# Weight slots of a split-precision transformer kernel: raw 6 to 4, high and low parts 3 to 4

## The reference

```python
for l in range(DEPTH):                      # DEPTH = 2, first block
    h = rmsnorm(x, norm_mix[l])
    proj = h @ w_in[l]                      # 1024 x 5956
    ...                                     # rope, top-k attention, recurrence
    merged = sigmoid(ga) * (y_attn @ w_proj_attn[l]) + sigmoid(gb) * (y_hgrn @ w_proj_hgrn[l])
    x = x + merged @ w_out[l]
    g, u = split(rmsnorm(x, norm_ffn[l]) @ w_ffn_in[l])     # 1024 x 5632
    x = x + (silu(g) * u) @ w_ffn_out[l]                    # 2816 x 1024
mod = silu(c) @ ada_w + ada_b               # second block: 1024 x 6144
...
x = x + g1 * rms_norm(hybrid_mixer(...))
x = x + g2 * rms_norm(swiglu_ffn(...))
```

## Time and profile before

| what | us |
|---|---|
| median of 3 runs | 1318.49 |
| the runs | 1316.56 to 1318.83 |
| the profiled execution, its own time | 1319.73 |
| span of that execution | 1317.9 |
| PE busy | 1213.8 |
| DVE busy | 849.3 |
| ACT busy | 616.0 |

### The profile page before, as it was taken

How to read it: one execution, slowest core, us unless ns; L and a number is a source line. 1 busy time by engine, 2 the same in 40 slices (tenths; PEclk the granted TensorE clock), 3 DMA queues, 4 the chain that set the end, 5 groups by cost and what they waited for, 6 DMA issues and landing times.

```text
span 1317.9 us, 21169 instructions
## 1 busy us (share of the span) xinstructions
PE 1213.8 (92%) x9046; PEld 1164.0 (88%) x9046; DVE 849.3 (64%) x1272; ACT 616.0 (47%) x738; POOL 0.2 (0%) x4
## 2 busy tenths in 40 slices
PE   5888978899999999789789999999899998999996
PEld 5678978899999987789789999999797887899996
DVE  6984463777676788844637776767775647644443
ACT  7565315464334355653154643343564347443343
POOL 0000000000000000000000000000000000000000
PEclk9999989999999999999899999999898798999998
DMA  9454322565868663544325658786443203455510
GB/s 346 124 174 128 128 96 65 170 214 173 273 228 278 212 207 91 179 128 128 96 65 179 205 178 270 240 273 214 154 146 110 96 1 128 160 189 171 184 65 33
DMA packets 177614, 214.15 MB, mean 162 GB/s; under 512 B 3696, under 2 KB 160752, under 8 KB 177520
## 3 DMA queue, kind: packets, MB, share of 16 engines
q1 hardware_dynamic: 176800, 211.86, 48.7%
q10 hardware_dynamic: 720, 0.94, 0.2%
HBM read 211.74 MB, written 1.05 MB: 161 GB/s over the span
## 4 chain that ended last, share of the span: by engine, by line
PE 72%; DVE 16%; ACT 8%; issue 3%; DMA 1%; SPq 0%; DVEq 0%; ACTq 0%
PE stream L492 16%; PE stream L493 15%; PE stream L494 15%; DVE w_lo L1304 6%; PE steps L494 4%; PE steps L493 4%; PE steps L492 4%; ACT w_hi L881 4%; PE steps L799 2%; PE steps L657 1%; PE stream L676 1%; ACT probs L881 1%; PE stream L580 1%; DMA raw<-in_w_in 1%; PE steps L647 1%
## 5 line engine op out<-in xcount | busy, mean ns | idle before, releaser
L1304 DVE TENSOR_TENSOR w_lo<-raw,w_hi 128x2048 fp32r<-128x2048 f32 (+2 forms) x178 | 402.4, 2266 | 328.2 <-ACT w_hi L881 326.5
L881 ACT ACTIVATE w_hi<-raw 128x2048 fp32r<-128x2048 f32 (+2 forms) x178 | 336.6, 1894 | 415.1 <-PE stream L494 372.0
L492 PE MATMUL stream<-h_hi,w_hi 128*128 128x256 f32 x1576 | 454.4, 288 | 11.7 <-DVE w_lo L1304 6.0
L493 PE MATMUL stream<-h_lo,w_hi 128*128 128x256 f32 x1576 | 449.9, 285 | 0.0
L494 PE MATMUL stream<-h_hi,w_lo 128*128 128x256 f32 x1576 | 449.6, 285 | 0.0
L492 PEld LDWEIGHTS stream<-h_hi,w_hi 128*128 128x128 f32 x1576 | 307.0, 195 | 15.5 <-DVE w_lo L1304 7.8
L493 PEld LDWEIGHTS stream<-h_lo,w_hi 128*128 128x128 f32 x1576 | 306.9, 195 | 0.5 <-issue 0.5
L494 PEld LDWEIGHTS stream<-h_hi,w_lo 128*128 128x128 f32 x1576 | 306.5, 195 | 0.0
L492 PE MATMUL steps<-gu_hi,w_hi 128*128 128x256 f32 x528 | 149.5, 283 | 0.7 <-DVE gu_lo L1561 0.7
L493 PE MATMUL steps<-gu_lo,w_hi 128*128 128x256 f32 x528 | 149.4, 283 | 0.0
L494 PE MATMUL steps<-gu_hi,w_lo 128*128 128x256 f32 x528 | 149.4, 283 | 0.0
(11 more groups left out here) (286 smaller groups left out, 1706.7 us busy)
## 6 DMA issues: line engine op xcount, KB each, us to landing
raw<-in_w_ffn_in SPq DMA_DIRECT2D x66, 1024.0 KB, 5.2
raw<-in_w_in SPq DMA_DIRECT2D x54, 1024.0 KB, 6.0
raw<-in_w_ffn_out SPq DMA_DIRECT2D x33, 1024.0 KB, 6.7
ada_raw<-in_ada_w SPq DMA_DIRECT2D x24, 1024.0 KB, 5.3
raw<-in_w_out SPq DMA_DIRECT2D x8, 1024.0 KB, 5.0
raw<-in_w_proj_attn SPq DMA_DIRECT2D x8, 512.0 KB, 3.5
raw<-in_w_proj_hgrn SPq DMA_DIRECT2D x8, 512.0 KB, 4.6
raw<-in_w_o SPq DMA_DIRECT2D x4, 1024.0 KB, 4.9
```

Source lines behind the costliest of these rows:

```text
L492: pe.matmul(dst, w_h, x_h, start=start, stop=False, skip_group_check=True)
L493: pe.matmul(dst, w_h, x_l, start=False, stop=False, skip_group_check=True)
L881: return act.activation(out_, in_, func, **kw)
L1304: tt(wl[m % SPL][:, 0:n], raw[m % RAW][:, 0:n], wh[m % SPL][:, 0:n].bitcast(F32), ALU.subtract)\
```

## The change

The raw slots go from six to four, the high and low parts from three to four each. The memory is the same 96 KB of each partition, cut otherwise. `split_ahead()` now splits the unit four places ahead. Since one more unit has to be ready at the start, `mixer(0)` gets one more split on each engine: on ACT behind a wait for parameters, on DVE behind `setup_tables()`. `first_outs` keeps working on three units. SP's loads wait for the split of the unit four before rather than six before.

```diff
-RAW = 6
-SPL = 3
+RAW = 4
+SPL = 4
...
-    wh = [at(f"w_hi{i}", [P, 2048], F32R, 48 + 8 * i) for i in range(SPL)]
-    wl = [at(f"w_lo{i}", [P, 2048], F32R, 72 + 8 * i) for i in range(SPL)]
+    wh = [at(f"w_hi{i}", [P, 2048], F32R, 32 + 8 * i) for i in range(SPL)]
+    wl = [at(f"w_lo{i}", [P, 2048], F32R, 64 + 8 * i) for i in range(SPL)]
...
             m = cur[0]
-            cur[0] += SPL
+            cur[0] += 3
...
-            for i in range(SPL):
+            for i in range(3):
...
                 split(2)
                 act.wait_ge(par_in, 64)
+                split(3)
             step()
             split_ahead()
...
                 setup_rope()
                 split(2)
                 setup_tables()
+                split(3)
```

## The result

| | before | changed |
|---|---|---|
| median of the runs, us | 1318.47 (1316.56 to 1318.83, 4 runs) | 1327.2 (1327.11 to 1328.34, 4 runs) |
| ratio | | 1.0071, 95% interval 1.0054 to 1.0089 |
| profiled execution, us (its span) | 1319.73 (1317.9) | 1327.29 (1325.5) |
| mean granted clock of TensorE | 0.953 | 0.946 |

The changed kernel is 8.7 us (0.7%) slower. I had forecast +4.7 us, with 1326.5 us as the upper end of the range. The sign was right. The time lies 0.7 us outside the range.

What follows compares the result with a forecast made beforehand. The prediction took PE to set the time over most of the kernel and DVE in two stretches. Its terms, 2.7 + 2.3 + 0.8 - 1.1 = +4.7 us, gave 1323.2 us on the median, range 1320.0 to 1326.5 us.

Steps and rivals of the forecast that it cites:

- What bounds the kernel: PE over most of the kernel, DVE in two stretches; PE's 10.6 us of `w_lo` waits there taken as worth 0 us.
- Rival (a): In DVE's two stretches, the extra ready unit pays: PE regains 10.6 us, net -5.9, 1312.6 us; chance 7%.
- what stays: PE's stops for something behind a split on DVE, for example in the recurrence, stay as they are; no change in time.
- First and second term: At the start, ACT's added split delays the cosine by 2.7 us; DVE's added split delays the rotation by 2.3 us more.
- rival (c): At the start, unit 4 lands late, its packets mixed with unit 5's: +7.4 us, 1325.9 us; chance 12%.
- Both terms go to the end: The start's 2.7 and 2.3 us pass through DVE to PE's softmax stop and the kernel's end: +5.0 us.
- rival (b): DVE's extra split at the start, 2.3 us, is hidden before the first softmax: +2.4 us, 1320.9 us; chance 15%.
- Third term: At block 0's end, the split ahead of the additions to `xT` grows from 1.50 to 2.29 us: +0.8 us.
- Fourth term: At block 1's end, the split ahead of the additions to `xT` shrinks from 2.28 to 1.22 us: -1.1 us.
- The loads: Loads issued two units later still land in time in the feed-forward parts: 0 us.
- Rival (d): Loads come too late in the feed-forward parts: +10 us and more, 1333 us; chance 3%.

Runs made afterwards that it cites:

- the pair with the decays first: DVE's two decays of each recurrence level moved ahead of that level's split, nothing else: 1290.7 us on the kernel before (three slots), 1302.4 us on the changed kernel (four).
- The pure delay on the kernel before: The kernel before with DVE's six writes of the rope tables made six times over instead of once, slots and splits untouched: 1326.0 us, ratio 1.0053.

## Why the prediction was right or wrong

- **What bounds the kernel: right.** PE's waits for `w_lo` in DVE's stretches were worth nothing. They became waits for `k_tm`, 7.20 us in block 0 and 5.41 us in block 1 (0.67 us of the 4.9 in block 0 lay at 23.26 us, ahead of the stretch in which the prediction put them all), and in the pair with the decays first the fourth slot gave nothing back. Rival (a) falls. The rule of the Trainium skill on gaps (page Perfetto Trace Analysis, section Identifying Performance Opportunities), cited there, found nothing for `w_lo`; its other half, to find what blocks the engine and make that come sooner, fits `hgrn_k`, 20.8 us of waits that became 3.7, which I had left among "what stays".
- **First and second term: right in size.** +2.46 us at the cosine and +4.66 at the rotation, against 2.7 and 5.0. Unit 4 was not late, so rival (c) falls. Each alone was worth what it was priced at, 2.6 and 2.2 us.
- **"Both terms go to the end": half right.** They reach the softmax at 100.82 us (101 forecast); PE's stop there is 2.99 us, not 3.42. But 2.34 us are given back by 142 us, and not by cover as in rival (b). So block 1's first matmul came at 476.26 us and block 2's at 937.96 us, not near 479 and 941. Behind the stop PE's clock was 0.66 before, and is 1.00 in the changed kernel (PE busy for 5.00 of 5.00 us in both, 32 matmuls against 44):

```profile
97.00:102.00 5.00, 5.00 (x32) 5.00 (x30) 4.08 (x8) 3.75 (x5) 0.00 (x0) 0.66 0.12 18
```
```profile
102.00:107.00 5.00, 5.00 (x44) 5.00 (x43) 4.39 (x9) 3.44 (x5) 0.00 (x0) 1.00 0.17 30
```

  This is no law. The pure delay on the kernel before lost 1.3 us more in the same place. Of the seven traces whose start is the changed kernel's, four give back 1.5 us between 92 and 107 us and three nothing; and the other 0.9 us, between 107 and 142 us, also come back in the second trace of the kernel before. So a part of these 2.3 us is chance of the two executions compared, and no term of mine foresaw it.
- **Third term: right,** +0.78 against +0.8.
- **Fourth term: the step that failed.** PE's stop at the head of block 2 did get 1.06 us shorter, as the term has it, and I counted that as -1.1 us. Its worth was -1.1 + 5.6 = +4.5 us, through TensorE's clock in block 2. The prediction took every stretch behind a shift to last as long as before. It read the granted clock as a property of the stretch, while here it changed when two stretches moved by 1 us against each other. Without the 5.6 us the profiled execution would have been at 1321.7 us, within the range. Why a shift of 1 us does this stays open.
- **The loads: right for the change,** with no wait for them in the feed-forward parts, but by a margin that three slots don't have. Rival (d) falls.
- **The size.** 4.7 forecast; 4.66 - 2.34 + 0.79 - 1.07 + 5.62 and -0.06 at other places in the traces (7.6), and 8.7 between the medians, since the traced execution of before was 1.3 us above its median. Single runs of the kernel before spread by 12 us, more than the effect; the interval of the ratio, 1.0054 to 1.0089, is what leaves no doubt of the sign. The range reached 1326.5 us because all its ends were waits; none was the clock.

## What to carry to other kernels

Price a change by the waits, but where the clock is not at 1.00 on both sides of a moved edge, put some microseconds in either direction into the range, and look at two traces before explaining one. Making weights ready earlier helps only the engine that is really late: look instead at what stands queued behind a wait in the engine that feeds it. Here one moved line was worth 28 us and a slot nothing.

## What was not expected of the hardware

The same 1153 matmuls of block 2 took 192.5 to 198.8 us, at a granted clock of 0.88 to 0.85 and with PE idle for 14.6 to 15.2 us in all of the stretches shown. A shift of 1.06 us at its head went with 5.6 us more, in six traces of six. Added idle work of 0.9 us made the kernel 2.7 us faster, and 2.0 us of it made it 4 us slower.
